# Scattering the experts' rows on the chip, and the final norm in front of the loop over crowded experts

## The chip, the core and the metric

The kernel runs on one core of a Trainium2 chip, as one program launched once. The metric is the device time of that launch in microseconds, the median of several executions. TensorE (PE in the profile) multiplies matrices into eight PSUM banks, VectorE (DVE) and ScalarE (ACT) do elementwise work, GpSimd (POOL) does small work and issues some transfers, SyncE (SP) issues the transfers of the weights. All transfers of the core run on its 16 DMA engines. Each engine has its own instruction queue, which it works off in order, and they meet at semaphores.

## What is computed

Two layers over 256 tokens of width 1024: a mixer of four head groups, then a channel mixer (dense in the first layer, the best two of eight experts for each token in the second), and a final norm. The change touches what follows the experts in the second layer:

```python
def moe_ffn(x, w_router, wg, wu, wd):
    ...
    gates = jnp.sum(jax.nn.one_hot(top_i, N_EXPERTS, dtype=jnp.float32) * w[..., None], axis=1)
    y = jnp.zeros_like(xt)
    for e in range(N_EXPERTS):
        y = y + gates[:, e:e + 1].astype(xt.dtype) * swiglu(xt, wg[e], wu[e], wd[e])
    return y.reshape(B, S, D)
...
            h = h + moe_ffn(hn, moe_router[l // 2], moe_w_gate[l // 2], moe_w_up[l // 2],
                            moe_w_down[l // 2])
    return rms_norm(h, final_norm)
```

All values are float32. The weights of the eight experts are 352 MB of the 444 MB that the core moves.

## The kernel before

**The experts.** The kernel sorts the experts by how many tokens chose them and gives each a place `e` from 0 to 7. Even places are wide: they hold up to 128 rows (`SLOTS`), and their products are taken in three fp32r passes, for which ACT and DVE split each piece of weights into a high part (`part_h`, three buffers) and a low part (`ring_l`, `more_l`, `part_l` and so on). Odd places are narrow: up to 64 rows (`FEW`), multiplied in plain fp32 straight from the loaded weights (operands `xn` and `hTn`). The 3584 hidden columns of an expert are done in two chunks, which makes 16 steps, wide and narrow in turn. The tokens of an expert are gathered by a product with a 0/1 matrix (`gm`, tile `xs`), and its output rows land in `ye` (tile `y` in the profile), copied out of PSUM by ACT in `moe_out`. Narrow outputs stand folded: columns 0 to 511 in partitions 0 to 63, the rest in partitions 64 to 127.

**The pieces.** `MOE_ORDER` lists 368 pieces of 0.75 or 1 MB: gate (part 0), up (part 1), and down (part 2) of the step before. All engines walk through this list by the piece's number `j`. PE computes piece `j` and then whatever a table hangs on it (`TURN_AT`, `GATHER_AT`, `GATES_AT`). ACT and DVE walk with `p = j - 3`: they do the side work of piece `p`, then split piece `j`. SP issues the load of a piece as soon as PE has used the piece that lay in its buffer before; there are 13 buffers. So the loads are held back by PE, and PE is held back by the loads, with up to 13 pieces between the two.

**The experts' outputs.** For places 0 to 6, POOL waits for `ye` and stores it to DRAM (`parked`). When all seven are stored, POOL fetches for each token the row of its first and of its second expert with four indirect transfers (`fetch`), whose row numbers and gates DVE has worked out in `token_rows`. DVE adds the four blocks of 128 tokens to the residual `h` (`add_fetched`). Place 7 alone is scattered on the chip: PE turns its gate matrix `gg` (`turn_gates_last`), ACT copies it to `ggT`, and after the last piece PE multiplies `ye` by it (`scatter_last`) into four banks that DVE adds to `h` (`add_last`).

**Crowded experts.** A loop of three turns follows (`MAX_OVER`), for experts with more tokens than slots. With these inputs no expert is crowded, so each turn is a compare and a branch around a long body. DVE, ACT and PE meet this loop after the scatter of place 7, SP already after its last load. Behind it come the final norm and the stores: ACT takes the squares of `h` ahead of the loop, DVE signals POOL behind the loop, POOL takes the root for both blocks, DVE writes `xs` in three pieces, SP stores them.

Of the kernel before, what the change touches and what calls it, by code (L numbers as in the profile page):

```python
# [12 lines left out]
P = 128  # L13
# [19 lines left out]
def hybrid_trunk(nc, x, positions, rope_inv, attn_norm, w_in, mla_q_norm, mla_w_uq, mla_kv_norm, mla_w_ukv,  # L33
# [107 lines left out]
    def rows_before(a):  # L141

        return sum((FEW if NARROW[i] else SLOTS) for i in range(a))

# [4 lines left out]
    def parks_before(a):  # L149

        return sum((2 if NARROW[i] else 1) for i in range(a))
# [9 lines left out]
    with ExitStack() as ctx:  # L161
# [79 lines left out]
        with nc.sbuf_tensor("fetch", [P, 2 * NB, D], F32) as fetch:  # L241
            pass
# [95 lines left out]
        row_at_rank = sb("row_at_rank", [P, E])  # L338
        rank_cmp = sb("rank_cmp", [P, E, E])
        rank_hot = sb("rank_hot", [P, E, E])  # L340
        row_base = sb("row_base", [P, E])
# [3 lines left out]
        stays = sb("stays", [P, E])  # L345
# [8 lines left out]
        gm = sb("gm", [P, NB, P])  # L354
        gg = sb("gg", [P, NB, P])
# [5 lines left out]
        keep = sb("keep", [P, NB, E])  # L361
        kval = sb("kval", [P, NB, E])
        ksel = sb("ksel", [P, 2, NB, E])
        kgate = sb("kgate", [P, 2, NB])
        krow_f = sb("krow_f", [P, 2, NB])
        krow = sb("krow", [P, 2, NB], mybir.dt.uint32)
        parked = nc.dram_tensor("parked", [rows_before(E - 1), D], F32).ap()
        fetched = [fetch[:, n, :] for n in range(2 * NB)]
# [139 lines left out]
        m_park = sem("moe_out_parked")  # L508
        m_row = sem("token_rows_known")
        m_fetch = [sem(f"token_rows_fetched{n}") for n in range(2 * NB)]  # L510
        m_comb = sem("token_rows_added")
# [159 lines left out]
        GATE_SHARES_AT = MOE_AT[1, 5, 2]  # L671
        ROWS_KNOWN_AT = MOE_AT[1, 9, 2]
# [16 lines left out]
        OUT_PARTS = ((0, 0, D), (1, 0, W), (1, W, W))  # L689
# [57 lines left out]
        def _(sp):  # L747
# [121 lines left out]
            load_experts()  # L869
            sp.wait_ge(s_over, 1)  # L870
# [5 lines left out]

            for i, (b, c, n) in enumerate(OUT_PARTS):
                sp.wait_ge(s_y, 2 * L + i + 1)
                sp.dma_start(out[0, b * P:(b + 1) * P, c:c + n], xs[:, b, c:c + n]).then_inc(s_out, 16)
            sp.wait_ge(s_out, 16 * len(OUT_PARTS))  # L880

        @block.gpsimd
        def _(pool):
# [38 lines left out]
            for r, a in enumerate(RANK_AT):  # L922
                pool.memset(rank_at[:, r:r + 1], float(a))
                pool.memset(row_at_rank[:, r:r + 1], float(rows_before(a)))
# [26 lines left out]
            for e in range(E - 1):  # L951
                pool.wait_ge(m_ye, e + 1)
                if NARROW[e]:
                    for side in range(2):
# [4 lines left out]
            pool.wait_ge(m_park, 16 * parks_before(E - 1))  # L959
            pool.wait_ge(m_row, 1)  # L960
            for n in range(2 * NB):
                k, b = divmod(n, 2)
                pool.indirect_dma_start(out=fetched[n], out_offset=None, in_=parked,
                                        in_offset=bass.IndirectOffsetOnAxis(ap=krow[:, k, b:b + 1], axis=0)
                                        ).then_inc(m_fetch[n], 16)
            pool.wait_ge(s_h, 2 * L)
            root(ms[:, 0:NB], rs[:, 0:NB], NB, s_rs)

        @block.tensor
        def _(pe):  # L970
# [633 lines left out]
            for j in range(NMOE):  # L1604
                moe_piece(j)
                if j == GATES_AT:
                    turn_gates_last()
# [1082 lines left out]
```

## Time and profile before

| | us |
|---|---|
| median of 3 executions | 1387.33 |
| lowest, highest | 1385.82, 1388.4 |
| the profiled execution | 1381.37 |
| its span, first to last instruction | 1379.6 |
| busy: PE 96%, DVE 54%, ACT 47%, POOL 3% of the span | |
| read from DRAM, written | 439.30 MB, 3.93 MB |

All times of rows are of the one profiled execution. A matmul's record starts when the matmul is issued, and its end is modelled: back to back matmuls overlap in the records, so their cost is the distance of their starts and not the duration shown. A plain fp32 matmul leaves two records, an fp32r matmul or a transpose one. Times run from the start of the span.

### The profile page before, as it was taken

What the parts mean: (1) busy time and instruction counts of PE and PEld (TensorE: products, weight loads), DVE (VectorE), ACT (ScalarE), POOL (GpSimd) and SP (SyncE); (2) the same over time, 40 slices, a digit from 0 to 9 for tenths busy, and PEclk for the clock granted to TensorE, in tenths of its full rate; (3) what the DMA queues carried; (4) which work ended last, traced back from release to release, by engine and by line L of the source; (5) the groups of instructions that cost most, each with busy time, mean ns of one, the idle gap of its engine ahead of it and who ended that gap; (6) DMA issues with size and microseconds to landing.
All of it is one profiled execution on the core that took longest, in us unless ns stands there. A gap on an engine that the chain in (4) does not pass through costs nothing.

```text
span 1379.6 us, 16481 instructions
## 1 busy us (share of the span) xinstructions
PE 1329.1 (96%) x6528; PEld 946.0 (69%) x6528; DVE 746.6 (54%) x787; ACT 643.3 (47%) x751; POOL 35.5 (3%) x96
## 2 busy tenths in 40 slices
PE   7999999999999999999999999999989999989995
PEld 6877788888878777658478558478448568538561
DVE  4656544454455567547258367268247358327443
ACT  5465534444354646347157147067137157226341
POOL 2000000000000000000000000000000000000001
PEclk9999999999999999999999999999999999999998
DMA  9730855554535649799999999999999999999995
GB/s 335 265 125 1 305 184 186 194 193 157 183 105 176 244 173 376 257 416 386 417 421 422 421 420 419 417 420 423 421 420 418 418 420 422 421 422 418 417 419 225
DMA packets 102031, 444.38 MB, mean 322 GB/s; under 512 B 9982, under 2 KB 22140, under 8 KB 71228
## 3 DMA queue, kind: packets, MB, share of 16 engines
q1 hardware_dynamic: 100388, 438.24, 80.6%
q0 software_dynamic: 1440, 4.98, 0.9%
q8 instruction: 54, 0.88, 0.3%
q14 instruction: 29, 0.24, 0.0%
q10 hardware_dynamic: 120, 0.04, 0.0%
HBM read 439.30 MB, written 3.93 MB: 321 GB/s over the span
## 4 chain that ended last, share of the span: by engine, by line
PE 85%; DMA 6%; ACT 4%; DVE 3%; issue 1%; POOL 0%; DVEq 0%; POOLq 0%; ACTq 0%; SPq 0%
PE bank L972 82%; DMA ring<-in_moe_w_down_dram 4%; PE bank L975 3%; DMA spare<-in_moe_w_down_dram 2%; ACT part_h L1634 1%; DVE ring_l L2037 1%; ACT xn L1634 0%; DVE nmax L2244 0%; ACT prob L1826 0%; ACT sg L1959 0%; ACT pxh L1634 0%; ACT in_h L1634 0%; ACT L1799 0%; ACT probT L1634 0%; DVE pxh L2037 0%
## 5 line engine op out<-in xcount | busy, mean ns | idle before, releaser
L1634 ACT ACTIVATE part_h<-ring 128x2048 fp32r<-128x2048 f32 (+1 forms) x124 | 224.4, 1816 | 161.4 <-PE bank L972 120.3
L972 PE MATMUL bank<-part_h,xh 128*128 128x512 f32 x688 | 271.2, 394 | 4.9 <-ACT sg L1959 2.0
L972 PE MATMUL bank<-part_h,xl 128*128 128x512 f32 x688 | 268.4, 390 | 0.0
L2037 DVE TENSOR_TENSOR ring_l<-ring,part_h 128x2048 fp32r<-128x2048 f32 (+1 forms) x82 | 170.8, 2095 | 82.5 <-ACT part_h L1634 82.2
L972 PEld LDWEIGHTS bank<-part_h,xh 128*128 128x128 f32 x688 | 129.3, 188 | 36.3 <-issue 7.3
L972 PEld LDWEIGHTS bank<-part_h,xl 128*128 128x128 f32 x688 | 129.1, 188 | 27.5
L2037 DVE TENSOR_TENSOR part_l<-ring,part_h 128x2048 fp32r<-128x2048 f32 x42 | 96.1, 2292 | 80.6 <-ACT part_h L1634 80.6
L972 PE MATMUL bank<-part_h,hTh 128*128 128x512 f32 x320 | 127.7, 399 | 11.7 <-DVE ring_l L2037 11.7
L972 PE MATMUL bank<-part_l,xh 128*128 128x512 f32 x335 | 130.3, 389 | 0.0
L2037 DVE TENSOR_TENSOR hTl<-bank,hTh 128x512 fp32r<-128x512 f32 x40 | 27.1, 690 | 183.4 <-ACT hTh L1634 183.4
L972 PE MATMUL bank<-part_h,hTl 128*128 128x512 f32 x320 | 126.1, 394 | 0.0
L1634 ACT ACTIVATE hTh<-bank 128x512 fp32r<-128x512 f32 x40 | 23.2, 596 | 187.6 <-PE bank L975 187.6
L2037 DVE TENSOR_TENSOR part_l<-part_in,part_h 128x2048 fp32r<-128x2048 f32 (+1 forms) x36 | 75.3, 2099 | 17.7 <-ACT part_h L1634 17.7
L972 PEld LDWEIGHTS bank<-part_h,hTh 128*128 128x128 f32 x320 | 61.1, 191 | 29.4 <-DVE ring_l L2037 15.2
L972 PE MATMUL bank<-ring,xn 128*64 128x512 f32 (+1 forms) x384 | 79.2, 548 | 1.1 <-DMA ring<-in_moe_w_up_dram 1.1
L1634 ACT ACTIVATE part_h<-part_in 128x2048 fp32r<-128x2048 f32 (+1 forms) x36 | 63.4, 1764 | 23.2 <-PE bank L972 23.2
L972 PE MATMUL bank<-ring_l,xh 128*128 128x512 f32 x186 | 72.4, 389 | 0.0
L972 PEld LDWEIGHTS bank<-part_l,xh 128*128 128x128 f32 x335 | 62.9, 188 | 12.7
L972 PEld LDWEIGHTS bank<-part_h,hTl 128*128 128x128 f32 x320 | 61.1, 191 | 13.0
L972 PE MATMUL bank<-in_h,pxh 128*128 128x512 f32 (+1 forms) x152 | 57.6, 379 | 0.5 <-DVE in_l L2037 0.5
L2037 DVE TENSOR_TENSOR most_l<-most,part_h 128x2048 fp32r<-128x2048 f32 (+1 forms) x25 | 52.5, 2099 | 8.3 <-ACT part_h L1634 8.2
L972 PE MATMUL bank<-in_l,pxh 128*128 128x512 f32 (+1 forms) x152 | 56.8, 374 | 0.0
(400 smaller groups left out, 2029.0 us busy)
## 6 DMA issues: line engine op xcount, KB each, us to landing
ring<-in_moe_w_down_dram SPq DMA_DIRECT2D x54, 1024.0 KB, 18.8
ring<-in_moe_w_up_dram SPq DMA_DIRECT2D x28, 1024.0 KB, 19.7
ring<-in_moe_w_gate_dram SPq DMA_DIRECT2D x22, 1024.0 KB, 21.4
ring<-in_moe_w_gate_dram SPq DMA_DIRECT2D x28, 768.0 KB, 17.8
part_in<-in_moe_w_down_dram SPq DMA_DIRECT2D x19, 1024.0 KB, 15.3
ring<-in_moe_w_up_dram SPq DMA_DIRECT2D x24, 768.0 KB, 15.7
part_in<-in_moe_w_up_dram SPq DMA_DIRECT2D x15, 1024.0 KB, 17.8
ring<-in_w_in_dram SPq DMA_DIRECT2D x7, 2048.0 KB, 8.1
```

The source lines that it names most:

```text
L972: return nc.tensor.matmul(o, lhsT, rhs, start=start, stop=stop)
L975: return nc.tensor.transpose(o, src, ident[0:n, 0:n])
L1634: return nc.scalar.activation(dst, src, ACT.Copy, scale=scale)
L2037: return nc.vector.tensor_tensor(o, a, b, op)
```

## The change

The stores to `parked`, the indirect fetches, `token_rows` and `add_fetched` are gone. Every place is now scattered on the chip. When a place's last down piece (`OUT_PIECE`) is done, DVE builds the gate matrix in `gate_slots`, PE turns it three pieces later (two 128x128 transposes), ACT copies it to `ggT`, and PE multiplies at 6, 8, 10 and 12 pieces behind `OUT_PIECE`, one 128x512 matmul each. DVE adds each result to `h` from the bank. The gate matrix of place 7 goes into `shift` (`ggT_last`) since it is turned ahead of its own use.

The final norm is written once ahead of the loop over crowded experts and once behind it, there only if an expert was crowded. ACT takes the squares block by block, POOL the root block by block, DVE multiplies `h` by the gain, ACT scales two of the three pieces by the root, DVE the third, into the buffer `more`, and SP stores them and waits for their landing ahead of its loop.

```diff
-            for e in range(E - 1):
-                pool.wait_ge(m_ye, e + 1)
...
-                        pool.dma_start(parked[rows_before(e):rows_before(e + 1), side * W:(side + 1) * W],
-                                       ye[side * FEW:(side + 1) * FEW, 0:W]).then_inc(m_park, 16)
-                else:
-                    pool.dma_start(parked[rows_before(e):rows_before(e + 1), :], ye).then_inc(m_park, 16)
...
-                pool.indirect_dma_start(out=fetched[n], out_offset=None, in_=parked,
...
+        GG_AT = {OUT_PIECE[e]: e for e in range(E - 1)}
+        GG_AT[OUT_PIECE[E - 3] + 5] = E - 1
...
+        GG_TURN_AT = {OUT_PIECE[e] + 3: e for e in range(E - 1)}
+        SCATTER_AT = {OUT_PIECE[e] + 6 + 2 * r: (e, r) for e in range(E - 1) for r in range(4)}
...
+            def scatter_moe(e, r):
+
+                b, half = divmod(r, 2)
                 if r == 0:
-                    pe.wait_ge(m_ye, E)
-                    pe.wait_ge(m_ggT, 1)
...
+                    pe.wait_ge(m_ye, e + 1)
+                    pe.wait_ge(m_ggT, E if e == E - 1 else GG_NTH[e] + 1)
+                    if e == E - 1:
+                        pe.wait_ge(m_add, 4 * e)
+                elif e < E - 1 and NARROW[e]:
+                    pe.wait_ge(m_add, 4 * e + r)
+                elif e < E - 1 and r >= 2:
+                    pe.wait_ge(m_add, 4 * e + r - 1)
...
+                mm(scatter_bank(e, r)[:, :], turned_, out_rows, True, True).then_inc(m_ysp, 1)
...
+                if j in GG_TURN_AT:
+                    turn_gates_moe(GG_TURN_AT[j])
+                if j in SCATTER_AT:
+                    scatter_moe(*SCATTER_AT[j])
...
+            def gate_slots(e):
+
+                past(dve, m_ggp, GG_NTH[e])
+                link(ts(eqm[:, :], place[:, :], float(e), None, ALU.is_equal))
...
+                        i = ts(gg[:, b, side * wide_:(side + 1) * wide_], iota_s[:, 0:wide_], col[:, b:b + 1],
+                               col[:, 2 * NB + b:2 * NB + b + 1], ALU.is_equal, ALU.mult)
+                i.then_inc(m_gg, 1)
...
+            def final_gain(n):
+
+                past(dve, s_out, 16 * OUT_STORES * n)
+                tt(gained[0], h[:, 0, :], fin_row[:, :], ALU.mult).then_inc(m_add, 1)
+                tt(gained[1][:, 0:W], h[:, 1, 0:W], fin_row[:, 0:W], ALU.mult).then_inc(m_add, 1)
+                dve.wait_ge(s_rs, L + NB * n + 2)
...
+            def final_scale(n):
+
+                for b in range(NB):
+                    act.wait_ge(m_add, ADDS + (7 if n else 2 * b + 2))
+                    square(h[:, b, :], D ** -0.5, ms[:, b:b + 1])
+                    squares_done(s_ms)
...
+                copy(gained[0], gained[0], rs[:, 0:1]).then_inc(s_ya, 1)
...
+            def store(n):
+
+                sp.wait_ge(s_ya, 2 * n + 1)
+                sp.dma_start(out[0, 0:P, :], gained[0]).then_inc(s_out, 16)
...
+                sp.wait_ge(s_out, 16 * OUT_STORES * (n + 1))
+
+            store(0)
             sp.wait_ge(s_over, 1)
             n_over = sp.value_load(over_i[0:1, 0:1], min_val=0, max_val=MAX_OVER)
             with sp.Fori(0, MAX_OVER) as i:
...
+            with sp.If(n_over > 0):
+                store(1)
```

How PE's queue reads in the last narrow step, whose up pieces (`xn`, into bank2 and bank3) and down pieces (`hTn`, into bank7) belong to place 7. Before:

```order
L972 MATMUL bank3<-most,xn 64x256 x2
L972 MATMUL bank2<-part_in,xn 64x512 x2
L972 MATMUL bank3<-part_in,xn 64x256 x2
L972 MATMUL bank2<-part_in,xn 64x512 x2
L972 MATMUL bank3<-part_in,xn 64x256 x2
L972 MATMUL bank2<-part_in,xn 64x512 x2
L972 MATMUL bank3<-part_in,xn 64x256 x2
L975 MATMUL bank6<-ident,sg 128x128 x4
L972 MATMUL bank7<-ring,hTn 64x512 x4
```

With the change, the same stretch:

```order
L972 MATMUL bank3<-most,xn 64x256 x2
L972 MATMUL bank2<-part_in,xn 64x512 x2
L972 MATMUL bank3<-part_in,xn 64x256 x2
L972 MATMUL bank5<-y,ggT 128x512
L972 MATMUL bank2<-part_in,xn 64x512 x2
L972 MATMUL bank3<-part_in,xn 64x256 x2
L972 MATMUL bank2<-part_in,xn 64x512 x2
L972 MATMUL bank3<-part_in,xn 64x256 x2
L972 MATMUL bank4<-y,ggT 128x512
L975 MATMUL bank6<-ident,sg 128x128 x4
L972 MATMUL bank7<-ring,hTn 64x512 x4
```

Two of the four scatter matmuls of place 6 (`y,ggT`) now stand between pieces of place 7. The same pattern stands once for each of the places 0 to 6, for 0, 2 and 4 in a wide step, for 1, 3, 5 and 6 in a narrow one.

DVE's queue in the wide step behind place 4, where `ring_l`, `most_l`, `pxh` and their like are the low halves that PE needs for its next pieces, with the change (before, the rows with `gg` and `h` are not there, nor the three rows ahead of `gg`):

```order
L2067 TENSOR_TENSOR most_l<-most,part_h 128x2048
L2071 TENSOR_SCALAR eqm<-place 128x8
L2067 TENSOR_TENSOR pick<-rsg,eqm 128x48
L2570 TENSOR_REDUCE col<-pick 128x6
L2072 TENSOR_SCALAR gg<-iota_s,col 128x128 x2
L2067 TENSOR_TENSOR ring_l<-ring,part_h 128x2048 x2
L2067 TENSOR_TENSOR most_l<-most,part_h 128x2048
L2067 TENSOR_TENSOR part_l<-part_in,part_h 128x2048 x3
L2067 TENSOR_TENSOR h<-h,bank5 128x512
L2067 TENSOR_TENSOR ring_l<-ring,part_h 128x2048 x2
L2067 TENSOR_TENSOR h<-h,bank4 128x512
```

The gate matrix and the adds stand ahead of splits in the same queue.

SP's queue behind the last load of weights, before:

```order
L854 DMA spare<-in_moe_w_down_dram 128x2048
L871 TENSOR_LOAD over_i
L871 ISA x2
L872 UNCONDITIONAL_BRANCH
L873 COMPARE_AND_BRANCH
```

and with the change:

```order
L850 DMA spare<-in_moe_w_down_dram 128x2048
L870 DMA out_dram<-more 128x1024
L872 DMA out_dram<-more 128x512
L874 DMA out_dram<-more 128x512
L879 TENSOR_LOAD over_i
L879 ISA x2
L880 UNCONDITIONAL_BRANCH
L881 COMPARE_AND_BRANCH
```

The three stores, and the wait for their landing, have moved from behind the loop to ahead of it.

## Rows read from the trace of the kernel before

**Rows 1.** Busy time by stretch: stretch, length, five engines, granted clock, DMA share, GB/s.
```profile
520.00:1355.00 835.00, 816.21 (x3893) 530.54 (x3894) 454.95 (x389) 386.94 (x348) 9.65 (x14) 0.99 1.00 410
```
**Rows 2.** Wait of SP's queue, 500 to 1380: total us, times, longest.
```profile
SPq L854 <- PE bank L972: 567.5, 318, 8.9
```
**Rows 3.** Timeline of PE: start, us, instruction, idle before it and what ended it.
```profile
1012.69 1.94 PE L972 MATMUL bank<-more,xn 128*64 128x512 f32 x8 [0.56 <-DMA more<-in_moe_w_up_dram]
...
1021.92 0.67 PE L972 MATMUL bank<-part_h,hTh 128*128 128x512 f32 x1 [4.81 <-DVE ring_l L2037]
...
1234.75 0.79 PE L972 MATMUL bank<-part_h,hTh 128*128 128x512 f32 x1 [4.82 <-DVE ring_l L2037]
```
**Rows 4.** Busy time by stretch, behind the two long waits of rows 3.
```profile
1021.00:1027.00 6.00, 5.08 (x15) 4.04 (x16) 5.81 (x5) 3.31 (x3) 0.00 (x0) 0.72 1.01 419
1233.00:1242.00 9.00, 7.25 (x20) 5.73 (x21) 7.38 (x5) 5.43 (x3) 0.00 (x0) 0.62 1.02 423
```
**Rows 5.** DMA queue 0 (POOL's: the parked rows and their fetches): packets, MB, share.
```profile
q0 software_dynamic: 1440, 4.98, 0.9%
```
**Rows 6.** Timeline of PE: where the gather into narrow places 3, 5 and 7 begins.
```profile
704.39 0.77 PE L972 MATMUL bank<-gm,xs 128*128 128x64 f32 x5
...
908.50 0.77 PE L972 MATMUL bank<-gm,xs 128*128 128x64 f32 x5
...
1120.97 0.77 PE L972 MATMUL bank<-gm,xs 128*128 128x64 f32 x5
```
**Rows 7.** Timeline of PE in layer 0: one plain fp32 matmul, and the next.
```profile
67.34 1.02 PE L972 MATMUL bank<-w_ukv,cT 128*128 128x512 f32 x2
68.20 1.45 PE L972 MATMUL bank<-w_uq,cT 128*128 128x384 f32 x4
```
**Rows 8.** Timeline of PE: turning the gate matrix of place 7 between narrow pieces.
```profile
1213.83 1.89 PE L972 MATMUL bank<-ring,xn 128*64 128x512 f32 x8
1215.65 0.44 PE L975 MATMUL bank<-ident,gg 128*128 128x128 f32 x2
1216.02 1.94 PE L972 MATMUL bank<-ring,xn 128*64 128x512 f32 x8
```
**Rows 9.** Chain that ended last: four transposes between wide pieces: start, us, what.
```profile
1261.59 0.47 PE bank L975 x4
```
**Rows 10.** Timeline of PE in the first wide up pieces, behind a slot matrix on DVE.
```profile
557.81 0.50 PE L972 MATMUL bank<-part_h,xh 128*128 128x512 f32 x1 [0.49 <-DVE ring_l L2037]
```
**Rows 11.** Timeline of all engines at the end.
```profile
1359.86 1.94 PE L972 MATMUL bank<-xT,hTn 128*64 128x512 f32 x8 [1.78 <-DMA xT<-in_moe_w_down_dram]
...
1363.59 1.94 PE L972 MATMUL bank<-spare,hTn 128*64 128x512 f32 x8 [1.79 <-DMA spare<-in_moe_w_down_dram]
...
1365.58 0.60 ACT L1634 ACTIVATE y<-bank 128x512 f32<-128x512 f32 x1 [12.63 <-PE bank L972]
...
1366.23 1.99 PE L972 MATMUL bank<-y,ggT 64*128 64x512 f32 x8 [0.70 <-ACT y L1634]
...
1367.47 2.66 DVE L2037 TENSOR_TENSOR h<-h,bank 128x512 f32<-128x512 f32 x4 [1.02 <-PE bank L972]
1369.56 1.06 ACT L1643 ACTIVATE junk<-h 128x1024 f32<-128x1024 f32 x1 [3.39 <-DVE h L2037]
...
1373.10 0.73 POOL L930 TENSOR_TENSOR rs<-ms,neghalf 128x2 f32<-128x2 f32 x1
1373.87 2.61 DVE L2661 SCALAR_TENSOR_TENSOR xs<-h,rs,fin_row 128x1024 f32<-128x1024 f32 x3 [3.74 <-POOL rs L930]
1375.18 1.67 SPq L879 DMA_DIRECT2D out_dram<-xs  x3
```
**Rows 12.** Loop over crowded experts: SP's by line, and PE's branch: ns min/median/max, first and last start.
```profile
L872 SPq MOVE  x4: 29/33/38, 1338.9 to 1345.3; - x4
L872 SPq ALU_OP  x3: 32/33/48, 1344.3 to 1345.7; - x3
...
L1618 PEldq COMPARE_BRANCH  x3: 221/233/3788, 1367.3 to 1372.4; - x3
```

More of the change, by code:

```diff
@@ L360, in hybrid_trunk @@
         lgT = ggT[:, :, :].rearrange("p b t -> p (b t)")
[L361 to L368, printed above, removed]
         hid = y[:, 1, :].rearrange("p (s n) -> p s n", s=2)
@@ L507, in hybrid_trunk @@
         m_add = sem("moe_added")
[L508 to L511, printed above, removed]
+        m_gg = sem("moe_gate_slots_ready")
+        s_ya = sem("scaled_by_scalar")
         m_once = sem("once_pieces_landed")
@@ L688, in hybrid_trunk @@
         EARLY = PARTS
-        OUT_PARTS = ((0, 0, D), (1, 0, W), (1, W, W))
+        OUT_STORES = 3
+        ADDS = 4 * (E - 1)
+        gained = [more[:, b * D:(b + 1) * D] for b in range(NB)]
         row_loads = []
@@ L2017, in _ @@
                     rows_from(i)
-                    act.wait_ge(s_yadd, i + 1)
-                    for b in range(NB):
-                        act.wait_ge(s_achain, i * NB + (squared + b))
-                        nc.scalar.activation(junk[:, 0:D], h[:, b, :], ACT.Square, scale=D ** -0.5,
-                                             accum_out=ms[:, b:b + 1]).then_inc(s_achain, 1)
-                    act.wait_ge(s_achain, i * NB + (squared + NB))
-                    act.sem_inc(s_ms, 1)
+            with act.If(n_over > 0):
+                final_scale(1)
         @block.vector
@@ L2568, in add_last, with add_moe @@
+            def add_moe(e, r):
+                dve.wait_ge(m_ysp, 4 * e + r + 1)
+                b, half = divmod(r, 2)
                 tt(h[:, b, half * W:(half + 1) * W], h[:, b, half * W:(half + 1) * W],
-                   bank[(6, 7, 4, 5)[r]][:, :], ALU.add).then_inc(m_add, 1)
+                   scatter_bank(e, r)[:, :], ALU.add).then_inc(m_add, 1)
             def expert_order():
@@ L2631, in _ @@
                     dve.wait_ge(m_xep, rounds_before(e))
-                    slots(e, place[:, :], m_gm, 2 if e == E - 1 else 0)
-                if j == NMOE - 1:
-                    add_fetched(0)
+                    slots(e, place[:, :], m_gm, 0)
                 if j in WIDE_N and EARLY <= j:
                     split_moe(j)
-            for n in range(1, 2 * NB):
-                add_fetched(n)
             dve.wait_ge(s_col, COLS * (E - 1))
-            dve.wait_ge(m_ggp, 1)
+            dve.wait_ge(m_ggp, E)
             link(tt(rsg[:, 0], rsg[:, 0], cap[:, None, :].to_broadcast(wide), ALU.subtract))
@@ L2655, in _ @@
                     add(i)
-            dve.wait_ge(s_ms, L + 1)
-            dve.sem_inc(s_h, 1)
-            dve.wait_ge(s_rs, L + 1)
-            for b, c, n in OUT_PARTS:
-                nc.vector.scalar_tensor_tensor(out=xs[:, b, c:c + n], in0=h[:, b, c:c + n], scalar=rs[:, b:b + 1],
-                                               in1=fin_row[:, c:c + n], op0=ALU.mult, op1=ALU.mult).then_inc(s_y, 1)
+            with dve.If(n_over > 0):
+                final_gain(1)
 _INS = ['x', 'positions', 'rope_inv', 'attn_norm', 'w_in', 'mla_q_norm', 'mla_w_uq', 'mla_kv_norm', 'mla_w_ukv',
```

161 lines of the change are left out of this document (78 added, 83 removed).

## The prediction

> **What bounds the kernel now.** I read the stretches first, to see which resource is full while the experts run. From 520 to 1355 us both are: the DMA engines are busy all the time at 410 GB/s, and PE is busy 816 of 835 us [rows 1]. The two hold each other through the 13 buffers. SP waited for PE to free a buffer 318 times, 567.5 us in all [rows 2], yet the DMA engines never ran dry, so those waits cost nothing. The question is which of the two is the longer one, and the waits of PE answer it. They are few: behind narrow steps PE ran out of landed weights twice, with 4.81 and 4.82 us in one piece and about 0.55 us twice ahead of each [rows 3]. The record blames DVE's split, but the split itself waited for its piece. Each of these waits also cost clock: the granted clock was 0.72 over 6 us and 0.62 over 9 us behind them [rows 4], which is 3.4 and 6.8 us at 1.2 GHz in place of 2.4.
>
> The cadence shows how close the two are. One pair of experts (a wide and a narrow one, 92 pieces, 88.1 MB) took 204.1 us from the gather at 704.39 to that at 908.50, where PE never waited for DMA. The next pair took 212.5 us, with such a wait [rows 6]. So PE needs 204 to 205 us for a pair. DMA needs 88.1 MB and 0.8 MB of parked rows at 420 GB/s (the rate beside the waits, [rows 4]), 211.6 us. Before the change DMA is the longer one by some 7 us a pair, and PE pays the difference in the two long waits and in two of 1.8 us at the end [rows 11].
>
> **What the change takes away.** The parked rows and their fetches are 4.98 MB [rows 5], 11.9 us at 420 GB/s. That brings DMA to 209.7 us a pair. POOL's waits and DVE's four adds of fetched blocks go too; they lay beside PE's work, the last two between 1363.8 and 1366.2, while PE's scatter of place 7 was under way, so I count them as nothing.
>
> **What it adds on PE.** For each of seven places PE gets four fp32 matmuls with 512 columns and two 128x128 transposes. No row shows such a matmul inside a wide step. The nearest is a plain one in layer 0: 67.34 to 68.20, 0.86 us from start to start [rows 7]. For the narrow places the contraction has 64 rows and not 128; I take the same 0.86, since the partner that could share the array stands two pieces away. Four transposes between wide pieces took 0.47 us of the chain [rows 9], so two are 0.24.
> - In a narrow step a switch costs more. Eight records of narrow weights take four slots of 0.43, so 1213.83 would be followed at 1215.55. The turned gates start at 1215.65, the next group at 1216.02, and its own first slot is 0.05 longer: 0.52 us for two transposes worth 0.24, so some 0.27 us go to breaking the pairing of the two column halves [rows 8]. I add 0.27 to each scatter matmul there: 1.13 us. A place scattered in a narrow step costs 4 x 1.13 + 0.52 = 5.0 us, and there are four (1, 3, 5 and 6): 20.2 us.
> - In a wide step matmuls do not run in pairs, so I add nothing: 4 x 0.86 + 0.25 = 3.7 us, three places (0, 2, 4): 11.1 us.
>
> The sum is **31.3 us** on PE. Its lower end is 7 x 3.7 = 25.9 us; 21 us if the narrow places ran at the 0.5 us a matmul that the scatter of place 7 shows (1.99 us for four, [rows 11]), but there the two row halves are neighbours. Its upper end is 7 x 5.0 = 35 us.
>
> **What it adds on DVE and ACT.** A gate matrix is five DVE instructions ahead of a split. The nearest event is the slot matrix at 554 us, also ahead of a split in a wide stretch: PE then waited 0.49 us [rows 10]. I take 0.4 us for each of the three wide places, 1.2 us. The adds (0.66 us each, [rows 11]) stand every second piece; DVE splits a piece in 2.3 us and PE now takes 2.7 plus the inserted matmul, so DVE catches up, and I count nothing. If it does not, the bound is 0.66 x 12 = 8 us. In narrow steps DVE and ACT have nothing to split and all of this is hidden. The new waits of PE for `m_add` are for adds whose result was due a piece earlier.
>
> **What PE gets back.** With 204.5 + 8.7 + 0.4 = 213.6 us a pair PE is now the longer one, against 209.7 for DMA. Its waits for weights should go:
> - two long waits and the short ones ahead of them, less the 0.43 us that such a transition costs anyway: 2 x 5.5 = 11.0 us
> - half clock behind them: 10.2 us in which the matmuls went at a little over half their pace, 4.8 us [rows 4]
> - at the end: the last two pieces of weights start 3.73 us apart where their work is 1.72 us, so 4.0 us [rows 11]
>
> That is **19.8 us** back.
>
> **The tail.** Before, from the copy of the last expert rows (1365.58) to the end it is 14.0 us. After, I place each step from that copy, T: first add at T+1.9 as before, the fourth done at T+4.6. Squares of block 0 behind the second add, of block 1 at T+4.7 to 5.8 (1.06 us each). POOL's root of block 0 by T+5.9, of block 1 by T+7.2 (about 1 us each). DVE's gains in between, its last piece T+7.3 to 8.0. ACT scales until T+7.9. The three stores are issued by T+8.8, where it was 1376.85, T+11.3, so the norm ends 2.5 us earlier. From there to the end it was 2.75 us, of which I give 0.35 to the closing instructions and 2.4 to the landing: T+11.2. But SP's loop now stands behind that landing. Before, it ran in the shadow of the last step, from 1338.9 to 1345.7, of which 5.4 us lie between its first instruction and the first behind the branch around the body (1344.3) [rows 12]. PE's same branch took 3.79 us with idle queues [rows 12]. I take 3.8 for SP, since its queues are idle too. Reading the count ahead of it is in no row here; I allow 0.7. Then 3.8, 1.5 for the other turns (1344.3 to 1345.7), 0.65 for the last branch and the closing: T+17.9. That is 3.9 us longer than before (0 if the jump costs nothing, +5.5 with 5.4 us).
>
> The Trainium skill says the same of such a jump (Runtime: NRT & Kernel Launch, Instruction fetch mechanics): a taken branch to code outside the two pages that the sequencer holds makes it wait for a fetch. It gives no time for it; the 3.8 and 5.4 us are the trace's, and they agree that the jump is slow.
>
> **The sum**: 31.3 + 1.2 - 19.8 + 3.9 = **+16.6 us** on the profiled execution, 1379.6 to 1396.2 us of span. The median shown lies 6 us over the profiled time; I carry the difference over: 1387.3 + 16.6 = 1403.9.
>
> **Rivals.**
> - *The array has room, and the DMA stream is what counts.* Then the added matmuls vanish and the end moves with the stream: -11.9 us, +3.9 for the tail: 1379. For it speaks that the DMA engines were busy throughout [rows 1]. Against it: in the undisturbed pair the matmuls were issued without a gap, so each added one moves all behind it. The Trainium skill gives this rival its strongest form (Perfetto Trace Analysis, Identifying the Most-Contended Engine): matmul busy time says little of headroom, the share of weight loads says more. By it PE was only 530 of 835 us busy [rows 1], with room for 31 us. Against that reading stand the counts: 3893 matmul records in 835 us are one every 0.21 us, and 0.21 us is what 512 columns take at 2.4 GHz.
> - *The price of a scatter is half of mine.* With 0.5 us a matmul throughout, PE's part is 16 us, and with a free jump the sum is 16 + 1.2 - 19.8 = -3; with my tail it is +1: 1384 to 1389. It needs the pairing of row halves that the code has pulled apart.
> - *More waits than I count.* If each add or gate matrix in a wide step delays a split (8 us) and SP's jump takes 5.4 us: +25, 1413. The same mechanism as the forecast, further out.
> - *DMA still binds in part.* The DMA lead would have to stay as thin as before though PE is slower by 9 us a pair. Then the long waits remain with 10 us: +26 as well. The lead can only grow when PE slows, so this is unlikely.
>
> **Chances.** The forecast with its own spread, about 1393 to 1412: 0.77. More waits, or DMA binding in part: 0.07. Half price, 1384 to 1389: 0.08, of which 0.03 lies below the bound of no change. The DMA stream alone: 0.08. A difference under 0.2% (2.8 us) can't be told from none here. Faster by more than that: 0.08 + 0.03 = 0.11, within it 0.05, slower 0.84. The range goes from 1393 (PE's part at its lower end with the jump at half its price) to 1412, and leaves out the stream, the half price and the far end of the waits.
>
> **What would show it.** Right: PE has no wait for DMA over 0.2 us after 700, the clock stays at 1.0 from 600 to the end, the distance of the gathers of rows 6 is 212 to 215 us twice, the DMA share falls below 1.0 in some stretches, the scatter matmuls add 0.86 us in wide and 1.1 in narrow steps, and SP's last instructions come some 6 us behind the landing of the stores. Wrong: gathers 205 us apart (the array had room), waits of 5 us left (DMA binds), or waits of PE for `m_add` and splits.

## The result, and the profile after

| | before | after |
|---|---|---|
| median, us (7 executions each) | 1384.16 | 1393.49 |
| lowest, highest | 1380.62, 1388.4 | 1393.24, 1399.14 |
| the profiled execution | 1381.37 | 1393.31 |
| its span | 1379.6 | 1391.6 |
| T, the copy of the last expert rows | 1365.58 | 1373.62 |
| tail, from T to the end | 14.0 | 17.9 |

The changed kernel is slower: 1.0070 times the time before, 95% interval 1.0043 to 1.0096. The forecast was 1404 with a range of 1393 to 1412. Direction and mechanism held, and the size was too large: the median lies only 0.5 us above the lower end of the range, the medians are 9.3 us apart and the profiled executions 12.0, where the sum said 16.6. Executions of one kernel spread by the granted clock: of 67 further ones of the kernel before, taken beside the experiments, 49 took under 1386 us with a mean granted clock of 0.989 to 0.994, and 18 took longer, up to 1394, with 0.980 to 0.987.

The stretch of [rows 1], and the two places of [rows 4], in the profile after (stretch, length, five engines, granted clock, DMA share, GB/s):

```profile
520.00:1355.00 835.00, 829.24 (x3914) 533.29 (x3913) 474.62 (x436) 386.88 (x353) 0.00 (x0) 1.00 0.99 406
...
1021.00:1027.00 6.00, 6.00 (x28) 1.86 (x26) 2.05 (x3) 1.77 (x1) 0.00 (x0) 1.00 1.02 426
1233.00:1242.00 9.00, 9.00 (x38) 2.70 (x38) 4.27 (x4) 3.64 (x3) 0.00 (x0) 1.00 1.01 421
```

PE has 13 us more of busy time in the 835 us, the clock is at its upper level throughout, and the transfers are at 406 GB/s where they were at 410. The busy share of the DMA engines does not show this: taken by 100 us, it is between 1.00 and 1.02 from 600 to 1300 us in both kernels, although the transfers of the first pair of experts (692 to 905 us, and 692 to 896 before) ran at 414 and at 420 GB/s. The waits of PE in this stretch (580 to 1345 us; engine, line, waited for, total us, times, longest), first before, then after:

```profile
PE bank L972 <- DVE ring_l L2037: 11.7, 6, 4.8
PE bank L972 <- DMA ring<-in_moe_w_up_dram: 1.1, 2, 0.6
PE bank L972 <- ACT sg L1959: 0.7, 4, 0.2
PE bank L972 <- DMA more<-in_moe_w_up_dram: 0.6, 1, 0.6
PE bank L972 <- DMA most<-in_moe_w_up_dram: 0.5, 1, 0.5
```
```profile
PE bank L972 <- DVE ring_l L2067: 2.1, 4, 0.8
PE bank L972 <- ACT sg L1978: 0.7, 4, 0.2
```

Every wait for DMA is gone, the two of 1.8 us at the end of [rows 11] too, and with them the two of 4.8 us that had been put down to DVE's split. SP, which is held by PE's use of the buffers, waits more than in [rows 2] (same kind of row, 500 to 1395 us):

```profile
SPq L850 <- PE bank L972: 671.4, 354, 9.8
```

The gathers of places 2, 4 and 6 begin in the timeline of PE (start, us, instruction) at these times:

```profile
692.21 0.71 PE L972 MATMUL bank<-gm,xs 128*128 128x128 f32 x4
...
904.86 0.49 PE L972 MATMUL bank<-gm,xs 128*128 128x128 f32 x2
...
1117.56 0.38 PE L972 MATMUL bank<-gm,xs 128*128 128x128 f32 x1
```

That is 212.65 and 212.70 us for a pair of experts. From the same starts it was 204.1 and 212.5 before. I call the first of them **G** and use it as the zero below: it lies between 692.0 and 693.3 us in all profiled executions but that of e10, at 692.39 before and 692.21 after.

At the end, all engines (timeline; the last rows are SP's instructions by line: ns min/median/max, first and last start):

```profile
1373.62 0.60 ACT L1653 ACTIVATE y<-bank 128x512 f32<-128x512 f32 x1 [10.77 <-PE bank L972]
...
1375.43 2.48 DVE L2067 TENSOR_TENSOR h<-h,bank 128x512 f32<-128x512 f32 x4 [4.50 <-PE bank L972]
...
1377.95 1.82 DVE L2067 TENSOR_TENSOR more<-h,fin_row 128x1024 f32<-128x1024 f32 x2
1378.03 1.22 POOL L933 TENSOR_SCALAR ms<-ms 128x1 f32<-128x1 f32 x1 [861.00 <-ACTq L1667]
...
1381.45 0.35 SPq L870 DMA_DIRECT2D out_dram<-more  x1
1381.96 0.35 SPq L872 DMA_DIRECT2D out_dram<-more  x1
1382.35 0.77 SPq L874 DMA_DIRECT2D out_dram<-more  x1
```
```profile
L879 SPq TENSOR_LOAD <-over_i x1: 276/276/276, 1386.3 to 1386.3; - x1
...
L880 SPq MOVE  x4: 29/33/38, 1386.9 to 1390.6; - x4
L880 SPq ALU_OP  x3: 33/33/48, 1389.5 to 1391.0; - x3
```

The last store is started at T+8.7, 2.2 us earlier than before (T+10.9). Its landing releases SP at T+12.7, and then SP reads the count and takes its branches until T+17.7.

### The profile page after: what moved, and what is told of

The parts are those of the page before. It is cut to its first block, busy times and chain, and to the rows that moved or that the text cites. A ratio compares the mean times of both kernels' runs of the same rounds, so it can differ in the third digit from the quotient of the medians.

```text
span 1391.6 us, 16685 instructions
## 1 busy us (share of the span) xinstructions
PE 1353.3 (97%) x6598; PEld 953.3 (69%) x6598; DVE 764.9 (55%) x836; ACT 646.1 (46%) x760; POOL 27.5 (2%) x76
## 3 DMA queue, kind: packets, MB, share of 16 engines
HBM read 437.20 MB, written 1.05 MB: 315 GB/s over the span
## 4 chain that ended last, share of the span: by engine, by line
PE 91%; ACT 4%; DVE 3%; issue 1%; POOL 1%; ACTq 0%; POOLq 0%; DVEq 0%
PE bank L972 87%; PE bank L975 4%; ACT part_h L1653 1%; DVE ring_l L2067 1%; ACT xn L1653 0%; DVE nmax L2274 0%; ACT prob L1845 0%; ACT sg L1978 0%; ACT pxh L1653 0%; ACT in_h L1653 0%; ACT L1818 0%; ACT probT L1653 0%; DVE pxh L2067 0%; DVE in_l L2067 0%; DVE y L2250 0%
## 5 line engine op out<-in xcount | busy, mean ns | idle before, releaser
L972 PE MATMUL bank<-part_h,xh 128*128 128x512 f32 x688 | 275.6, 401 | 5.0 <-ACT sg L1978 2.0
L972 PEld LDWEIGHTS bank<-part_l,xh 128*128 128x128 f32 x335 | 62.9, 188 | 13.1 <-issue 0.5
L2067 DVE TENSOR_TENSOR h<-h,bank 128x512 f32<-128x512 f32 x44 | 29.6, 684 | 67.4 <-PE bank L972 67.3
## 6 DMA issues: line engine op xcount, KB each, us to landing
ring<-in_moe_w_down_dram SPq DMA_DIRECT2D x54, 1024.0 KB, 12.7
```

The costliest lines, as they stand in the source:

```text
L972: return nc.tensor.matmul(o, lhsT, rhs, start=start, stop=stop)
L2067: return nc.vector.tensor_tensor(o, a, b, op)
```

## The experiments

Each run below is compared with the kernel before on the same chip. Where two profiled executions are compared, I use G to T, the two pair distances and the tail:

| run | pairs, us | G to T | tail | ratio to before, interval |
|---|---|---|---|---|
| before | 204.1, 212.5 | 673.2 | 14.0 | |
| after | 212.7, 212.7 | 681.4 | 17.9 | 1.0070 [1.0043, 1.0096] |
| e1 after again | 212.7, 212.7 | 681.5 | 18.0 | 1.0105 [1.0067, 1.0143] |
| e2 traffic back | 212.7, 212.7 | 681.5 | 18.0 | 1.0075 [1.0039, 1.0111] |
| e3 before, no traffic | 204.1, 209.5 | 664.0 | 14.0 | 0.9951 [0.9928, 0.9974] |
| e4 norm only | 204.2, 212.9 | 673.6 | 18.2 | 1.0023 [0.9996, 1.0050] |
| e5 loop in shadow | 212.7, 212.7 | 681.4 | 13.1 | 1.0061 [1.0034, 1.0089] |
| e6 scatters twice | 219.6, 219.6 | 705.6 | 18.2 | 1.0276 [1.0230, 1.0321] |
| e7 scatters in pairs | 210.1, 210.1 | 673.7 | 13.1 | 0.9992 [0.9970, 1.0015] |
| e8 and two edits more | 210.1, 210.1 | 671.7 | 13.1 | 0.9960 [0.9940, 0.9980] |
| e9 root first | 210.1, 210.1 | 671.6 | 13.2 | one execution, 1379.71 us |
| e10 e8, traffic back | 210.0, 210.0 | 672.1 | 13.1 | 1.0004 [0.9971, 1.0036] |

**e1, the changed kernel again.** No edit.

> The changed kernel once more, for a closer ratio on one chip. From the two profiled executions (1379.6 and 1391.6 us of span) I expect a ratio of 1.0087, between 1.006 and 1.010. If the 6 us by which the median of three stood over the profiled time was chance, the ratio comes out at about 1.009; if the kernel before has a slower median by nature, at about 1.005.

The median was 1394.94 beside 1383.47 for before, and the trace repeats the first to 0.1 us in every column. The ratio came out at 1.0105, just above the 1.006 to 1.010 expected; the two intervals overlap between 1.0067 and 1.0096. By the reading set down beforehand, the 6 us between the first median of three and the profiled time were chance.

**e2, the traffic put back.** The changed kernel with POOL's stores of the rows and four fetches of the same bytes (direct transfers here, indirect ones before), which nobody uses.

```diff
+            for e in range(E - 1):
+                pool.wait_ge(m_ye, e + 1)
...
+                    pool.dma_start(parked[rows_before(e):rows_before(e + 1), :], ye).then_inc(m_park, 16)
...
+            for n in range(2 * NB):
+                pool.dma_start(fetched[n], parked[n * P:(n + 1) * P, :]).then_inc(m_fetch, 16)
```

> The changed kernel, with the DRAM traffic put back: POOL stores the rows of places 0 to 6 as before, and fetches 4 blocks of 128 rows (with direct transfers, same bytes as the indirect ones), and nothing uses them. Theory (PE is the longer resource now, 212.7 us a pair against 209.7 for DMA without the traffic and 211.6 with it): the traffic is hidden, at most 1 to 2 us slower than the changed kernel, about 1392 us of span, and PE has few and short waits for weights. Rival (the DMA stream still sets the end): 4.98 MB at 420 GB/s, 12 us slower, about 1403 us.

G to T is 681.5 as without it, and PE has no wait for DMA. The 4.98 MB that the change takes away are worth nothing once PE does the scatter. This speaks against the rival in which the stream of bytes sets the end.

**e3, the kernel before without the traffic.** The stores, the fetches and the adds of the fetched blocks are left out; the contribution of places 0 to 6 is therefore missing from what it computes.

```diff
-            for e in range(E - 1):
-                pool.wait_ge(m_ye, e + 1)
...
-            for n in range(1, 2 * NB):
-                add_fetched(n)
```

> The kernel before, without the stores to DRAM, the fetches and the adds of fetched rows; it leaves out the contribution of places 0 to 6. Theory (before, DMA is the longer one): the end moves by the bytes, 12 us, to about 1368 us of span, and PE keeps about 10 of its 22 us of waits. Rival 1 (the traffic was hidden, and PE's matmuls alone set the time): no change, 1380 us. Rival 2 (the waits come all from the traffic): PE's waits go whole, 20 us or more, under 1360 us.

It is the other half of e2: here, where DMA is the longer one, leaving them out is worth 9.2 us from G to T, less than the 12 forecast by the bytes; so PE keeps more than the 10 us of waits that I had expected. (The profiled executions are 8.4 us apart, the medians 5.7.) Of the 9.2 us, 5.4 come from the two transitions to a wide step and 3.8 from the very end. The two long waits have shrunk but not gone (timeline of PE, idle time in brackets; beside 4.81 and 4.82 in [rows 3]):

```profile
1019.83 0.50 PE L957 MATMUL bank<-part_h,hTh 128*128 128x512 f32 x1 [3.66 <-DVE ring_l L2021]
...
1230.64 0.80 PE L957 MATMUL bank<-part_h,hTh 128*128 128x512 f32 x1 [4.42 <-DVE ring_l L2021]
```

Of the two waits of 1.8 us at the end ([rows 11]) one of 0.2 is left (waits of PE, 580 to 1380 us):

```profile
PE bank L957 <- DMA spare<-in_moe_w_down_dram: 0.2, 1, 0.2
```

**e4, the norm in front of the loop, alone.** The kernel before with the new roots, gains, scales and stores, and SP's loop behind the stores.

```diff
-            root(ms[:, 0:NB], rs[:, 0:NB], NB, s_rs)
+            final_roots(0)
...
+            store(0)
             sp.wait_ge(s_over, 1)
...
-            for i, (b, c, n) in enumerate(OUT_PARTS):
```

> The kernel before with the second half of the change alone: the norm in front of the loop, block by block, and SP's stores and the wait for them in front of its loop. Theory: the norm itself ends 1 to 2.5 us earlier, but SP's loop of 4.8 us now follows the landing, so +3.5 to +4 us, 1383 us of span. Rival (the norm in front of the loop is a gain, as the scatter's price hides it): -2.5 us, 1377 us.

G to T is 0.4 us longer, the tail 4.2. So the tail's cost belongs to this part of the change and needs no scatter. This is read from the traces: the ratio of the medians, 1.0023, has an interval that includes 1. SP's rows show the same order as in the profile after:

```profile
L885 SPq TENSOR_LOAD <-over_i x1: 271/271/271, 1379.9 to 1379.9; - x1
...
L886 SPq ALU_OP  x3: 33/33/48, 1383.1 to 1384.5; - x3
```

**e5, SP's loop in the shadow.** The changed kernel with SP's loop ahead of the stores, as it was before the change.

```diff
-            store(0)
             sp.wait_ge(s_over, 1)
...
             with sp.If(n_over > 0):
-                store(1)
+                sp.wait_ge(s_ya, 4)
+                sp.wait_ge(s_y, 2 * L + 2)
+            store(0)
```

> The changed kernel with SP's loop over the crowded experts ahead of the stores again, so that its branch runs in the shadow of the last step; the rest as in the changed kernel. My theory: the tail of the changed kernel (17.94 us from the copy of the last expert rows, T, to the end) holds 3.7 us of reading the count, branch and closing of SP behind the landing of the stores (1386.3 to 1391.2 in the trace). With the loop ahead it is the landing plus some 0.4 us: T+13.2, 4.8 us less, span some 1387, and T where it was (1373.6 to 1374.0). Rival: the landing comes later too since another engine's branch (PE's or ACT's) ends last: then the tail stays above 15 us.

The tail falls from 17.9 to 13.1 us, as my theory had it, and G to T stays. The kernel is still 0.6% slower than the one before. The loops of the other engines still stand in the tail and end nothing: it closes 0.4 us behind the landing. (DVE's wait for free `gained` buffers, which matters only with crowded experts, is changed to fit.)

**e6, each scatter matmul twice.**

```diff
+                if e < E - 1:
+                    mm(scatter_bank(e, r)[:, :], turned_, out_rows, True, True)
                 mm(scatter_bank(e, r)[:, :], turned_, out_rows, True, True).then_inc(m_ysp, 1)
```

> The changed kernel with each of the 28 scatter matmuls of places 0 to 6 issued twice, one behind the other, into the same bank (the sum is the same). My theory: PE is the longer resource from the first scatter to the end, so each added matmul moves the end by its own 0.86 us: 28 x 0.86 = 24.1 us, up to 28 us if the second one of a narrow step costs the full 1.2: T about 1398 to 1402, span about 1416 to 1420, pairs of experts 212.7 + 6.9 = 219.6 us apart. Rival (the array has room, the stream of weights sets the pace): T moves by less than a third of that, under 8 us, and the pairs stay near 213.

G to T grows by 24.2 us, each pair by 6.9. The 28 added matmuls are 0.86 us each, and all of it arrives at the end. In the timeline of PE a doubled scatter in a wide step is one group of four records:

```profile
742.48 1.88 PE L972 MATMUL bank<-y,ggT 128*128 128x512 f32 x4
743.79 0.79 PE L972 MATMUL bank<-part_h,xh 128*128 128x512 f32 x1
```

The Trainium skill would have it otherwise (Perfetto Trace Analysis, Identifying the Most-Contended Engine): the busy time of matmuls says little of how close TensorE is to its limit, and it is to be judged by MFU, the share of the peak rate of arithmetic, and by the share of time in weight loads. I worked out only the second of the two. Weight loads were busy 533 of 835 us in the changed kernel, and yet each of the 28 added matmuls moved the end by its full price. For the weight loads the measurement decides against the page; on MFU no run here says anything.

**e7, the narrow scatters in pairs.** e5, and of a narrow place the two row halves stand side by side, into banks 5 and 4, at two places in the list instead of four. PE's wait for the add of the matmul before goes with it.

```diff
-            return bank[7] if NARROW[e] else bank[5 - r % 2]
+            return bank[5 - r % 2]
...
+                after_ = 7 + 2 * (r // 2) if NARROW[e] else 6 + 2 * r
```

> e5 with the four scatter matmuls of a narrow place in two pairs, the two row halves side by side, each pair into banks 5 and 4, in place of four matmuls in four pieces. My theory: a single one costs 1.2 us in a narrow step (0.86 plus the break of the pairing), a pair of row halves runs together at 0.5 us each as the scatter of place 7 does (1.99 us for four) plus one break of 0.3: 1.3 us a pair in place of 2.4. Three narrow places (1, 3, 5) and place 6 make 8 pairs: 8 x 0.9 to 1.1 = 7 to 9 us less than e5: T about 1366, span about 1379 to 1380, pairs of experts 2 x 1.0 shorter, some 210.7 us. Rival: if PE then runs ahead of the landed weights again, waits for DMA return and part of the gain goes into them: pairs above 211 and T above 1369. By the bytes DMA needs 209.7 us for a pair, so the two are nearly level.

Each pair of experts is 2.5 us shorter (forecast 2.0), G to T 7.7 us (7 to 9). That the second figure came is luck. The expectation counts eight pairs of matmuls, two of them of place 6, but the edit asks for `NARROW[e]`, and place 6 is wide: its matmuls stay single, and it costs 4.5 us as before. Only the six pairs of places 1, 3 and 5 changed, and each gave 1.28 us in place of 0.9 to 1.1. The single scatter of the changed kernel in a narrow step, and the one that follows two pieces on (timeline of PE):

```profile
800.24 1.94 PE L972 MATMUL bank<-spare,xn 128*64 128x512 f32 x8
802.11 1.12 PE L972 MATMUL bank<-y,ggT 64*128 64x512 f32 x2
803.16 1.94 PE L972 MATMUL bank<-more,xn 128*64 128x512 f32 x8
804.93 1.89 PE L972 MATMUL bank<-most,xn 128*64 128x512 f32 x8
```

and two of them in e7:

```profile
802.28 1.89 PE L977 MATMUL bank<-more,xn 128*64 128x512 f32 x8
804.10 1.13 PE L977 MATMUL bank<-y,ggT 64*128 64x512 f32 x4
805.16 1.94 PE L977 MATMUL bank<-most,xn 128*64 128x512 f32 x8
```

Two take 1.06 us from start to start where one took 1.05: the second is free when it uses the other half of the rows. The rival (waits for DMA return) did not come, though the pairs are now level with the 209.7 us that I had worked out for DMA.

**e8, two edits more.** e7, with the scatter of place 6 moved on to where PE waits for a product and for a turn in the last step, and two tiny operations of POOL just before its first root.

```diff
+                if e == E - 2:
+                    after_ = 8 + r // 2
...
+            pool.wait_ge(m_ye, E)
+            link(pool.tensor_scalar(warm_t[:, 0:1], neghalf[:, 0:1], 1.0, None, ALU.add))
+            link(pool.tensor_tensor(warm_t[:, 1:2], warm_t[:, 0:1], neghalf[:, 0:1], ALU.pow))
...
+                if (E - 2, 1) in SCATTER_AT.get(j, ()):
+                    scatter_moe(E - 2, 1)
```

> e7 with two more edits: the scatter of place 6 stands one piece later (its first two matmuls around the last turn, the other two in the piece behind), and POOL does two tiny operations when the last expert rows are copied, so that its first root doesn't come out of 860 us of idleness. My theory: the first root takes 0.23 and 0.73 us in place of 1.22 and 0.86 and the stores go out some 0.8 us earlier, tail about T+12.4 against T+13.2 in e7; T as in e7 or 0.5 less; span about 1378, ratio to the kernel before 0.998 to 1.0. Rival: the root waits for the squares anyway, tail as in e7.

It is the one version that beats the kernel before: 1379.00 beside 1382.64. But its gain over e7 came from the other edit than the one I had expected it from. G to T is 2.0 us shorter. Of this, 1.1 us come from one matmul that now stands in a wait of the last step, where it costs 0.1 us in place of 1.2: e7 has 0.69 us idle between the two rows below, and e8, behind it, has a scatter matmul there. Another 0.7 us come from the last two matmuls, which now stand side by side in the next piece and cost 1.7 us in place of 2.4. (The first one lay in a wait in e7 already.)

```profile
1351.42 0.63 PE L980 MATMUL bank<-ident,sg 128*128 128x128 f32 x4
1352.74 1.94 PE L977 MATMUL bank<-ring,hTn 128*64 128x512 f32 x8 [0.69 <-ACT hTn L1656]
```
```profile
1349.66 0.63 PE L987 MATMUL bank<-ident,sg 128*128 128x128 f32 x4
1350.12 1.02 PE L984 MATMUL bank<-y,ggT 128*128 128x512 f32 x2
1351.07 1.94 PE L984 MATMUL bank<-ring,hTn 128*64 128x512 f32 x8
```

The tail stayed at 13.1, and POOL's first root is as slow as ever behind 2.95 us of rest instead of 861. The idea that it wakes slowly has fallen.

**e9, the root first.** e8, and DVE starts its first product only when POOL's root of block 0 is done.

```diff
+                dve.wait_ge(s_rs, L + NB * n + 1)
                 tt(gained[0], h[:, 0, :], fin_row[:, :], ALU.mult).then_inc(m_add, 1)
```

> e8 with one wait added: DVE starts its first product of the final gain only when POOL's root of block 0 is done. It tells why POOL's first root instruction takes 1.2 us in e5 to e8 and in the changed kernel, where it took 0.23 us before the change. My theory after e8 (where two operations of POOL just ahead changed nothing): it isn't idleness, POOL is held up while DVE's product of 1.23 us runs beside it. Then the first root takes 0.2 + 0.6 us here (T+4.5 to T+5.4), and the hold moves to block 1: its root, due at T+5.6, is held until the product started at T+5.4 ends at T+6.7. Rival (the first root is slow by itself, from waking on a semaphore): it takes 1.1 to 1.2 us again with DVE idle. The stores go out later than in e8 either way, since the products come later: tail 13.5 to 14.5 us.

Timeline of DVE and POOL, e8 first, then e9:

```profile
1368.26 1.83 DVE L2080 TENSOR_TENSOR more<-h,fin_row 128x1024 f32<-128x1024 f32 x2
...
1368.42 1.14 POOL L942 TENSOR_SCALAR ms<-ms 128x1 f32<-128x1 f32 x1 [2.95 <-ACTq L1680]
```
```profile
1369.26 0.22 POOL L942 TENSOR_SCALAR ms<-ms 128x1 f32<-128x1 f32 x1 [2.95 <-ACTq L1680]
1369.56 0.57 POOL L943 TENSOR_TENSOR rs<-ms,neghalf 128x1 f32<-128x1 f32 x1
...
1370.23 1.82 DVE L2080 TENSOR_TENSOR more<-h,fin_row 128x1024 f32<-128x1024 f32 x2 [1.17 <-POOL rs L943]
1370.51 1.03 POOL L942 TENSOR_SCALAR ms<-ms 128x1 f32<-128x1 f32 x1 [0.38 <-ACTq L1680]
```

With DVE idle the root takes 0.22 and 0.57 us. The hold moves to block 1, whose first operation takes 1.03 us beside the product. ACT's squares of block 1 ran beside POOL's first operation in both runs, so they are not what holds it. In e4 the product was half done when POOL's first operation began (1372.13, the product from 1371.44 to 1372.67), and it took 0.63 us. So a product of DVE with both inputs in SBUF holds up POOL's next operation until it is done. The Trainium skill states this rule (SBUF — State Buffer, Who interferes with whom: DVE and GpSimd share a pair of ports as an exclusive lock, and a DVE instruction with two SBUF inputs contends with a GpSimd operation that reads SBUF). The trace agrees; I had not looked for it. The tail is 13.2, a little better than the 13.5 to 14.5 expected.

**e10, e8 with the traffic back.** The edit of e2, on e8.

> e8 with the stores of the expert rows (places 0 to 6) and four fetches of the same bytes added back, unused. In the changed kernel this cost nothing (e2), since PE was the longer one by 3 us a pair of experts. In e8 a pair takes 210.1 us, where DMA needs 209.7 without the traffic and 211.6 with it. My theory: DMA is the longer one again, PE's waits for weights return, T is 4 to 7 us later than in e8 (1368 to 1371), more if half clock follows a long wait, span some 1381 to 1385. Rival (the stream has slack that 420 GB/s does not show, or the lead of landed weights covers it): T within 1 us of e8 and the traffic was never worth removing, in any form of the scatter.

My theory fell. G to T is 672.1, 0.4 us more than in e8, and all of it is one wait in the very last piece, 0.24 us idle and 0.4 by the distance of the starts (timeline of PE):

```profile
1368.67 1.94 PE L1010 MATMUL bank<-spare,hTn 128*64 128x512 f32 x8 [0.24 <-DMA spare<-in_moe_w_down_dram]
```

The profiled execution reached G 6.4 us late, after half clock long before the experts, which the comparison from G leaves out. The medians with their wide interval (1383.62, from 1379.29 to 1391.89) settle nothing here. From 692 to 1320 us the transfers ran at 420 GB/s, as my estimate has it, and not faster. By the bytes DMA was then 1.5 us a pair slower than PE, some 6 us over the four pairs, and the lead of landed weights covered it. That the lead shrank shows in the time from issue to landing of the loads issued from 1300 to 1345 us (KB each, median us), in e8 and in e10:

```profile
ring<-in_moe_w_down_dram SPq DMA_DIRECT2D x7, 1024.0 KB, 15.6
```
```profile
ring<-in_moe_w_down_dram SPq DMA_DIRECT2D x8, 1024.0 KB, 20.4
```

In the kernel before the deficit was 7 us a pair by the same estimate, some 13 us from 620 us, where the transfers first ran at over 400 GB/s, to the first wait at 1010.

## Why the prediction was right, and where its size was off

**What bounds the kernel: right.** PE and the stream were within some per cent, and the added matmuls made PE the longer one. e3 shows that the stream was the longer one before, e2 and e6 that PE is after.

**PE's added work, 31.3 us forecast, 30.2 measured.** From G on, both traces hold the same 3108 matmul records once the scatters and the turned gates are set aside. So each record can be laid beside its own in the other kernel, and what is added or falls away shows as a step in their distance. A wide place costs 3.57 us where the sum had 3.7, a narrow one 4.99 (5.0), and three of each are 25.7. Place 6 costs 4.5, since one of its four matmuls stands where PE waits for a product anyway. A scatter matmul in a narrow step costs 1.2 us (800.24 to 803.16 in the rows above, less four slots of 0.43), a little more than the 1.13 of the sum. The gates' turns cost 0.17 at places 1, 3 and 5 and not 0.52, since they stand beside other transposes.

**Delays of the splits, 1.2 us forecast, none seen.** PE's waits for `ring_l` are 2.1 us in 4 places after, and these stand at the change from a narrow to a wide step in both kernels. A gate matrix of five small instructions ahead of a split found enough slack, although a slot matrix at 554 us had not ([rows 10]). Why the one delays PE and the other does not I did not test.

**What PE gets back, 19.8 us forecast, 21.9 measured: the step of the sum that failed.** G to T grew by 8.2 with 30.2 added. The direction was right and the term too small. The mis-sized part is the price of the two long waits and the short ones ahead of them: 11.0 us in the sum, 13.3 measured. I took the idle times of [rows 3] and subtracted 0.43 us for a transition. But the idle time shown is already less than what a wait costs. The rows of the kernel before show it in their starts (timeline of PE):

```profile
811.08 0.50 PE L972 MATMUL bank<-part_h,hTh 128*128 128x512 f32 x1
...
1008.21 1.89 PE L972 MATMUL bank<-xT,xn 128*64 128x512 f32 x8
1010.20 1.94 PE L972 MATMUL bank<-spare,xn 128*64 128x512 f32 x8
...
1015.17 1.94 PE L972 MATMUL bank<-most,xn 128*64 128x512 f32 x8 [0.55 <-DMA most<-in_moe_w_up_dram]
```

A narrow piece takes 1.72 us. From 1010.20 to 1012.69 it took 2.49, 0.77 more, where the row shows 0.56 idle; and up to 1010.20 it was 1.99, 0.27 more, with no idle shown. Over the whole approach: from the gather of [rows 6] to the first matmul of the wide step it is 106.7 us without a wait (704.39 to 811.08), and 113.4 and 113.8 in the next two pairs (to the rows 1021.92 and 1234.75 of [rows 3]; the last holds 0.5 for the turned gates of [rows 8]). The waits cost 6.7 and 6.6 us, not 5.5. The other two parts nearly cancel in their errors: with the records side by side the half clock cost 1.6 us behind the first long wait and 2.7 behind the second, 4.3 where the sum had 4.8, and the end 4.3 where it had 4.0. Together 6.7 + 6.6 + 4.3 + 4.3 = 21.9.

**The tail, +3.9 forecast, +3.9 measured, by luck: two errors cancel.** SP's jump took 2.5 us (1387.1 to 1389.5) and not 3.8, and the landing came at T+12.7 and not T+11.2. Reading the count (0.7) and the other turns (1.5) were as forecast. The last store was started at T+8.7, but SP took 0.77 us to issue it where it had taken 0.34, so the stores were issued by T+9.5 and not by T+8.8. And each took longer to land (DMA issues at the end: KB each, median us from issue to landing), before and after:

```profile
out_dram<-xs SPq DMA_DIRECT2D x1, 512.0 KB, 2.7
out_dram<-xs SPq DMA_DIRECT2D x2, 256.0 KB, 2.7
```
```profile
out_dram<-more SPq DMA_DIRECT2D x1, 512.0 KB, 3.2
out_dram<-more SPq DMA_DIRECT2D x2, 256.0 KB, 3.7
```

They are issued 0.9 us apart from first to last where it was 1.3, so they share the DMA engines for longer; I did not test that. I had carried over the 2.4 us of the last one as if it were a fixed delay. Nor had I seen that DVE's product would hold POOL's root by 1 us. Of the jump the rows show 2.5 us here and in e4, 3.8 for PE, and 5.4 for SP while it had loads in flight ([rows 12]; 5.2 from the branch itself). e5 shows that putting it back costs nothing and saves 4.8 us.

**The profiled execution: 1396.2 forecast, 1391.6 measured**, 4.6 less: 1.1 on PE, 1.2 on the splits, 2.1 on what comes back, and 0.2 because G came earlier.

**From there to the median: 6 us too high, the largest error of all.** The median of three executions lay 6.0 us over the profiled one, and I carried this over as if it belonged to the kernel. It was mostly chance: 49 of the 67 further executions of the kernel before were shorter than the shortest of those three. With more executions the median before is 1384.16 and 1383.47, 2 to 3 us over the profiled time, and after the change median and profiled time are nearly the same (1393.49 and 1393.31). More than half of the miss of 10.4 us is this.

**The range.** Its lower end does not follow from what it is said to hold: PE's part at 25.9 and the jump at half its price, with the other terms, give 1396.6. It takes a free jump and no delay of the splits to come to 1393. The median fell between the two, so that it lies in the range is luck as well.

**The signs that I had named.** These came: no wait for DMA, clock at 1.0, gathers 212 to 215 us apart twice, 0.86 us for a scatter matmul in a wide step (742.33 to 743.42 for one and a regular matmul of 0.23), and SP's end 5.2 us behind the landing. The 1.1 us in narrow steps is 1.2. One did not come: the DMA share stayed at 1.00 or above, and only the rate fell, so this share would not have told the forecast from its rivals.

## What to carry to other kernels

Work moved from the DMA side to PE pays back the DMA's excess only once, and from the point where PE is the longer one each added matmul costs its full price: here the trade was 22 us of waits for 30 us of matmuls. Before such a change is dropped, look at where the new matmuls stand: in pairs of row halves and in the waits of the last step, and with SP's loop put back in the shadow, the same scatter beats the kernel before by 0.4% (e8). A control loop that does nothing still cost 4.8 us behind the stores, of which 2.5 are one jump, so it belongs where its engine waits anyway. And a forecast that starts from the profiled execution is compared with it, or with a median of many: the offset of a median of three was worth more here than any term of the sum was wrong.

## What the runs showed of the hardware

- An idle time in the record is less than what a wait costs: 0.56 us idle was 0.77 us between starts, and 0.27 us were lost where no idle was shown. Only the same instructions elsewhere in the trace give the price.
- An fp32 matmul of 128x512 costs 0.86 us between fp32r matmuls of 0.23. Alone among column-paired narrow ones it costs 1.20, and a second one on the other row half is free (1.06 us from start to start for one and for two).
- A DVE product with two SBUF inputs holds a tiny POOL operation until it is done: 1.22 us in place of 0.22 where both begin together, 0.63 where the product is half done (e4).
- The busy share of the DMA engines was 1.00 to 1.02 at 414 GB/s as at 420, so it did not show which kernel had DMA to spare.
- A deficit of the weight stream of 1.5 us a pair, over four pairs, left one wait of 0.24 us (e10), while the loads near the end took 20.4 us from issue to landing where they took 15.6 without the deficit (e8). What decided here was the deficit times its duration against the lead, and not which rate is lower; both deficits are estimates from bytes and 420 GB/s.
